# Hybrid decoder step with a product-key expert layer: expert weights through a table in device memory instead of one-hot matrix products

## The chip, the cores and the metric

One core of a Trainium2 chip. The time is device microseconds of one execution. The kernel before took 1174.33 us, the median of three runs (1173.85 to 1175.8).

## The reference

The reference is one layer of a decoder for 256 prompt tokens and 8 sample tokens: attention beside a state-space branch, an output projection, and an expert layer (PEER). All but the last part is the same in both kernels. The expert layer is this, for each token `xb` and each of 8 heads:

```python
qh = (xb @ wq).reshape(c, PEER_HEADS, 2, PEER_QDIM // 2)
s = einsum('chid,hikd->chik', qh, sub_keys)            # two lists of 128 scores
sv, si = top_k(s, 16)                                   # 16 best of each list
cand = sv[:, :, 0, :, None] + sv[:, :, 1, None, :]      # 256 sums
best, bi = top_k(cand, 16)                              # 16 best sums
e = i1 * 128 + i2                                       # their expert numbers
g = softmax(best)
act = gelu(einsum('cd,chkd->chk', xb, u_emb[e]))
out = einsum('chk,chkd->cd', g * act, v_emb[e])
```

There are 128 x 128 = 16384 experts, each with a row of 1024 numbers in U (`u_emb`) and in V (`v_emb`). A token takes 8 x 16 = 128 of them.

## The kernel before

The program runs in blocks: first the token mixing (input projection by a ring of weight tiles, attention, the state-space scan, output projection), then, from about 300 us, the block of the expert layer, which is all that the change touches apart from some transfers.

**Prompt tokens are computed densely.** For the 256 prompt tokens the kernel doesn't gather expert rows. It multiplies all tokens by all of U, applies gelu, multiplies each result by a weight that is zero for experts which the token didn't choose, and multiplies by all of V. Expert number c x 128 + p stands in row c and partition p of `acts`, a buffer of 128 partitions by 128 rows by 256 tokens.

- *U sweep* (`up`, L1689): 128 rows, each 24 matrix products of 128 x 256. U arrives on SP's queue in 256 pieces of 256 KB (two a row) in a ring of 8 places. Each piece is split into a rounded high half and the rest: ScalarE makes the high half (`high`, L1805), GpSimd the low one by a subtraction (`low`, L1567), in `hl`, which has four places. So ScalarE can be no more than four pieces ahead of TensorE. ScalarE then applies gelu to the row (L1872).
- *V sweep* (`down`, L1719): 32 groups of four rows, each 48 products of 128 x 512 which add up in four banks. V comes in 8 pieces a group. GpSimd makes six of the low halves and VectorE two (L2092). The weighted `acts` rows are split too, by ScalarE (L1901) and VectorE (`parts`, L2085).

**The search** is VectorE's. It takes the 16 best of 128 and then the 16 best of 256, head by head (`choose`, `top16`, L1978 to L1988), for both tiles of 128 tokens at once, then a ninth time for the sample tokens. A last stage (L2003 to L2031) turns the positions into expert numbers and the scores into softmax weights for all nine heads together; the exponential is ScalarE's, put behind row 44 of the sweep (L1891). From row 60 of the U sweep on (`R0`), TensorE turns these numbers so that a token is a column (L1774), and then works a group of four tokens (`TG`) after each row of U:

- VectorE (`one_hots`, L2047 and L2051) compares the numbers of each token with 0 to 127 and gets two 128 x 128 matrices, one for the low half of the expert number, one for the high half times the weight;
- TensorE (`route`, L1699) multiplies the two, which gives the dense 128 x 128 weights of the token, for four tokens in a bank;
- VectorE (`weigh`, L2060) multiplies the rows of `acts` that exist already, ScalarE keeps the rest for later rows (`keep`), and VectorE weighs each later row as it comes (`finish`, L2068).

The 64 groups go with rows 60 to 123. When all is weighted, TensorE adds the residual (L1739) and starts the V sweep. Sample tokens are done apart: their rows of U and V are fetched by 16 indirect gathers of 128 rows, issued by GpSimd in groups 12 to 15 and 21 to 24 of the V sweep (L1577).

## Time and profile before

| | |
|---|---|
| median of three runs | 1174.33 us (1173.85 to 1175.8) |
| the profiled execution, first to last instruction | 1177.8 us |
| TensorE busy | 1145.5 us |
| VectorE busy | 793.4 us |
| GpSimd busy | 758.9 us |
| ScalarE busy | 569.8 us |
| U sweep, first product to the last | 381.5 to 802.8 us |
| V sweep | 807.5 to 1171.3 us |

The profile is of one execution, and no time of it other than its span is given; the span is 3.5 us above the median. Engines in it: PE is TensorE, DVE VectorE, ACT ScalarE, POOL GpSimd, SP the engine that issues most transfers. "L1719" is line 1719 of the kernel. A timeline row gives start, duration, engine, line, operation, output and input, and in brackets how long the engine had been idle and what ended that.

### The profile page before, as it was taken

The numbers are of one execution on the slowest core, as the hardware profiler recorded it, in microseconds if no ns is written. First come the engines' busy times: TensorE is split into PE (matmuls) and PEld (weight loads), VectorE is DVE, ScalarE is ACT, GpSimd is POOL, SyncE is SP. The second block draws the span as 40 slices with busy tenths as digits, with TensorE's granted clock in tenths as the row PEclk, the third lists the DMA queues.
The fourth block names the chain that finished last, engine by engine and source line by source line (L and its number), as shares of the span: only waits on it lengthen the run. The fifth ranks groups of instructions, "written<-read, shape, count | busy, mean of one in ns | idle before, by whom it ended". The sixth has DMA issues, their size and how long they took to land.

```text
span 1177.8 us, 24286 instructions
## 1 busy us (share of the span) xinstructions
PE 1145.5 (97%) x7599; PEld 1012.2 (86%) x7599; DVE 793.4 (67%) x1718; ACT 569.8 (48%) x1289; POOL 758.9 (64%) x642
## 2 busy tenths in 40 slices
PE   8999999989999999999999999999999999999997
PEld 7887777758888999999999999998888887888876
DVE  6789788874299997002899999984454466665534
ACT  3323223544354555565555554445555555555545
POOL 0066443237355998988666666676677797789754
PEclk9999999999999999999999999999999999999999
DMA  7468667695443666656544455545666697788653
GB/s 249 143 231 280 195 194 221 207 344 175 152 155 109 199 186 185 187 172 189 143 144 139 141 143 144 144 143 153 187 188 189 189 325 252 224 281 291 191 153 108
DMA packets 108667, 225.13 MB, mean 191 GB/s; under 512 B 12754, under 2 KB 21570, under 8 KB 108074
## 3 DMA queue, kind: packets, MB, share of 16 engines
q1 hardware_dynamic: 104706, 210.50, 57.5%
q0 software_dynamic: 2944, 10.49, 2.6%
q10 hardware_dynamic: 936, 3.14, 0.7%
q8 instruction: 41, 0.67, 0.3%
q14 instruction: 40, 0.33, 0.1%
HBM read 215.80 MB, written 8.19 MB: 190 GB/s over the span
## 4 chain that ended last, share of the span: by engine, by line
PE 71%; issue 1%; DVE 1%; POOL 0%; ACT 0%; DVEq 0%; POOLq 0%; ACTq 0%
PE bank L1689 31%; PE bank L1719 30%; PE bank L1699 5%; PE bank L1642 2%; PE bank L1654 1%; PE bank L1666 1%; DVE hl L2092 0%; PE bank L1739 0%; PE bank L1756 0%; POOL hl L1582 0%; DVE acts L2115 0%; PE bank L1747 0%; ACT acts L1925 0%; POOL hl L1567 0%; PE bank L1774 0%
## 5 line engine op out<-in xcount | busy, mean ns | idle before, releaser
L1567 POOL TENSOR_TENSOR hl<-ring,hl 128x512 fp32r<-128x512 f32 x448 | 585.5, 1317 | 187.5 <-ACT hl L1805 180.5
L1805 ACT CAST hl<-ring 128x512 fp32r<-128x512 f32 x512 | 317.1, 620 | 292.1 <-PE bank L1719 161.7
L1689 PE MATMUL bank<-split,hl 128*128 128x256 f32 x3072 | 378.5, 282 | 0.4 <-ACT hl L1805 0.3
L1689 PEld LDWEIGHTS bank<-split,hl 128*128 128x128 f32 x3072 | 366.3, 189 | 0.8 <-issue 0.5
L1719 PE MATMUL bank<-hl,split 128*128 128x512 f32 x1524 | 353.9, 394 | 1.9 <-DVE hl L2092 1.9
L1719 PEld LDWEIGHTS bank<-hl,split 128*128 128x128 f32 x1524 | 286.2, 188 | 69.7 <-DVE hl L2092 2.4
L533 PE MATMUL pj<-xn,ring 128*128 128x264 f32 x672 | 158.5, 392 | 0.7 <-ACT proj L824 0.7
L2085 DVE TENSOR_TENSOR split<-acts,split 128x256 fp32r<-128x256 f32 x128 | 128.3, 1028 | 40.0 <-ACT split L1901 37.0
L533 PEld LDWEIGHTS pj<-xn,ring 128*128 128x128 f32 x672 | 126.4, 192 | 24.7 <-issue 4.6
L2092 DVE TENSOR_TENSOR hl<-ring,hl 128x512 fp32r<-128x512 f32 x64 | 49.9, 779 | 115.6 <-ACT hl L1805 115.6
L2051 DVE TENSOR_SCALAR bv<-bkey,ig 128x130 f32<-128x130 f32 x256 | 86.0, 394 | 0.0
L2060 DVE TENSOR_TENSOR acts<-acts,bank 128x244 f32<-128x244 f32 (+31 forms) x64 | 66.3, 1035 | 19.7 <-PE bank L1699 19.4
L471 POOL TENSOR_TENSOR hs<-hs,dds 128x256 f32<-128x256 f32 x32 | 21.1, 689 | 87.8 <-DVE xdt L1266 45.7
L1872 ACT ACTIVATE acts<-bank 128x256 f32<-128x256 f32 (+31 forms) x124 | 40.9, 330 | 67.5 <-PE bank L1689 67.5
L1699 PE MATMUL bank<-bv,av 128*128 128x128 f32 x512 | 67.4, 275 | 0.0
L515 POOL TENSOR_TENSOR wo<-ring,wo 128x512 fp32r<-128x512 f32 x32 | 42.9, 1358 | 31.1 <-ACT wo L973 31.0
L1699 PEld LDWEIGHTS bank<-bv,av 128*128 128x128 f32 x512 | 62.4, 191 | 0.0
L1582 POOL TENSOR_TENSOR hl<-ring,hl 128x512 fp32r<-128x512 f32 x24 | 31.0, 1301 | 35.9 <-ACT hl L1815 35.8
L1901 ACT CAST split<-acts 128x256 fp32r<-128x256 f32 x128 | 51.2, 402 | 0.2 <-DVE acts L2068 0.2
L2068 DVE TENSOR_TENSOR acts<-acts,gtmp 128x256 f32<-128x256 f32 (+32 forms) x67 | 41.8, 624 | 8.4 <-ACT gtmp L1874 8.4
L2047 DVE TENSOR_TENSOR av<-bank,ig 128x512 f32<-128x512 f32 x64 | 43.4, 678 | 0.0
L1642 PE MATMUL bank<-split,hl 128*128 128x264 f32 x288 | 37.3, 288 | 0.0
(369 smaller groups left out, 1107.1 us busy)
## 6 DMA issues: line engine op xcount, KB each, us to landing
ring<-in_uv SPq DMA_DIRECT2D x256, 256.0 KB, 2.7
ring<-in_v_rows SPq DMA_DIRECT2D x256, 256.0 KB, 3.1
ring<-in_w_ring SPq DMA_DIRECT2D x76, 512.0 KB, 4.2
room<-in_cache_k SPq DMA_DIRECT2D x64, 128.0 KB, 2.8
hs<-in_state_ssm SPq DMA_DIRECT2D x8, 512.0 KB, 4.7
out_ssm_s<-hs SPq DMA_DIRECT2D x8, 512.0 KB, 6.3
acts<-x_rows SPq DMA_DIRECT2D x8, 512.0 KB, 4.7
room<-in_cache_v SPq DMA_DIRECT2D x12, 256.0 KB, 5.7
```

The costliest lines, as they stand in the source:

```text
L533: mm = nc.tensor.matmul(pj[i % 2][:, 0:NT], ring[:, s, k], (xg if i < 2 else xn)[:, k], start=(k == 0), stop=(k == KD - 1))
L1567: nc.gpsimd.tensor_tensor(hl[:, r % HL, 1], raw[:, r], hl[:, r % HL, 0].bitcast(F32), ALU.subtract).then_inc(lo_done, 1)
L1642: mm = nc.tensor.matmul(qb[s][:, 0:NT], hl[:, n % HL, m, k * P:(k + 1) * P], split[:, x, 4 * a + k], start=(a + kind + k == 0), stop=(a + ...
L1689: mm = nc.tensor.matmul(out, hl[:, r % HL, m, k * P:(k + 1) * P], split[:, x, kk, 0:TP], start=(kk == 0 and n == 0), stop=(kk == KD - 1 an ...
L1699: mm = nc.tensor.matmul(rb[m % 2][:, j * P:(j + 1) * P], av[:, m % 2, j], bv[:, m % 2, j, 0:P], start=True, stop=True)
L1719: mm = nc.tensor.matmul(acc[2 * k + half][:], split[:, p, 2 * s + a, k * P:(k + 1) * P], hl[:, r % HL, m], start=False, stop=False)
L1805: nc.scalar.copy(hl[:, r % HL, 0], raw[:, r]).then_inc(hi_done, 1)
L1901: nc.scalar.copy(split[:, g % 2, 2 * n, 0:TP], acts[:, g * GRP + n, :]).then_inc(wg_hi, 1)
L2051: hot = nc.vector.tensor_scalar(bv[:, m % 2, j], bkey[:, :, 0:BW // BR], ig[:, 0, at:at + 1], ig[:, 2, at:at + 1], ALU.is_equal, ALU.mult)
L2060: nc.vector.tensor_tensor(a, a, rb[m % 2][:].rearrange("p (t c) -> p t c", t=TG)[:, :, 0:R0 + m + 1], ALU.mult).then_inc(g_out, 1)
L2085: nc.vector.tensor_tensor(split[:, p, 2 * s + 1, 0:TP], acts[:, g * GRP + s, :], split[:, p, 2 * s, 0:TP].bitcast(F32), ALU.subtract).then ...
L2092: nc.vector.tensor_tensor(hl[:, r % HL, 1], raw[:, r], hl[:, r % HL, 0].bitcast(F32), ALU.subtract).then_inc(lo_dve, 1)
```

## The change

The dense weights are no longer computed by products. They are added up in a table `gates` in device memory: 16384 experts by 256 tokens of 4 bytes, 16.8 MB.

- *Clearing.* Behind the last 32 of the 52 tiles of the input projection ScalarE's queue issues a transfer of zeros, 512 KB each, in runs of 1 KB (`clear_gates`).
- *Search in two parts.* After head 4 VectorE makes expert numbers and weights of heads 0 to 4 (`gate_weights`), then goes on with heads 5 to 7, the sample tokens and their numbers and weights. The exponentials stand behind rows 13 and 60 (`EA`, `EB`). A token's place in the table is (number x 256 + token), in `slot`.
- *Scattering.* For each head, tile and one of its 16 choices GpSimd issues an indirect transfer which adds 128 numbers of 4 bytes (one a token) to the table: 8 x 2 x 16 = 256 transfers. The 16 of a head and tile wait until those of the head before have landed for this tile.
- *Low halves.* GpSimd makes only the first 32 of U's low halves (`PA`); the other 224 are VectorE's, two behind each step of the search from head 5 on, one at places, and from piece 152 on in a loop (`up_lows`). GpSimd scatters meanwhile.
- *Weighing.* Before each group of four rows in the V sweep, SP's queue reads the group's 512 KB of the table into `gt` (two places, runs of 1 KB), and VectorE multiplies the four rows at once. The first such read waits for all the scatters.
- Gone are `one_hots`, `route`, `keep`, `finish` and the turning of the prompt tokens' numbers; only the sample tokens' are still turned, after row 75 (`RT`).

```diff
-TG = 4
-NTG = TP // TG
+RZ = 4
...
-R0 = 60
-BR, BW = 5, 130
-C_ID, C_ONE, C_IOTA, C_LAST, C_ROPS, C_AM, C_CM = np.cumsum([0, P, P, P, NT, NT, 3 * P]).tolist()
+R0 = 64
+RT = 76
+HA = 5
+PA = 32
+EA, EB = 13, 60
...
+                def clear_gates(n):
+                    act.wait_ge(zeros_set, 1)
+                    rows = t["gates"].rearrange("(c p t) o -> p c (t o)", p=P, t=TP)[:, n * RZ:(n + 1) * RZ]
+                    act.dma_start(rows, zeros[:].unsqueeze(1).broadcast_to([P, RZ, TP])).then_inc(gates_zero, 16)
...
+                    if i >= N_IN - NKEY // RZ:
+                        clear_gates(i - N_IN + NKEY // RZ)
...
+                    stream(1, PA // RAW + 1)
+                    stream(PA // RAW + 1, RT // 4 - 1)
+                    sp.wait_ge(g_done, 2 * TT)
+                    sp.wait_ge(found_done, 4 * TT)
...
+                    def gate_tile(g):
+                        if g >= 2:
+                            sp.wait_ge(weighed, g - 1)
+                        rows = t["gates"].rearrange("(c p t) o -> p c (t o)", p=P, t=TP)[:, g * GRP:(g + 1) * GRP]
+                        sp.dma_start(gt[:, g % 2], rows).then_inc(gt_in[g % 2], 16)
...
+                    for k in range(TT):
+                        sp.wait_ge(scattered[k], 16 * TOPK * PH)
+                    gate_tile(0)
+                    gate_tile(1)
...
+                    def scatter(h, k):
+                        if h:
+                            pool.wait_ge(scattered[k], 16 * TOPK * h)
+                        for s in range(TOPK):
+                            nc.gpsimd.indirect_dma_start(t["gates"], bass.IndirectOffsetOnAxis(ap=slot[:, k, h, s:s + 1], axis=0),
+                                                         found[:, 2, k, h, s:s + 1], None, compute_op=ALU.add).then_inc(scattered[k], 16)
...
-                    with pool.Fori(0, N_U // RAW) as i:
+                    with pool.Fori(0, PA // RAW) as i:
                         for r in range(RAW):
                             low(i * RAW + r, r)
+                    pool.wait_ge(gates_zero, 16 * NKEY // RZ)
+                    for h in range(PH):
+                        if h in (0, HA):
+                            n = 1 if h == 0 else 2
+                            pool.wait_ge(g_done, TT * n)
+                            pool.wait_ge(slot_done, TT * n)
+                        for k in range(TT):
+                            scatter(h, k)
...
-                    def route(m):
-                        if m >= 2:
-                            pe.wait_ge(g_kept, m - 1)
-                        pe.wait_ge(g_b, m + 1)
-                        for j in range(TG):
-                            mm = nc.tensor.matmul(rb[m % 2][:, j * P:(j + 1) * P], av[:, m % 2, j], bv[:, m % 2, j, 0:P],
-                                                  start=True, stop=True)
-                        mm.then_inc(g_mm, 1)
...
+                    with pe.Fori(1, PA // RAW) as i:
                         for j in range(4):
-                            up(i, j)
-                    pe.wait_ge(found_done, 4)
-                    pe.wait_ge(g_done, 2)
+                            up(i, j, lo_done, 0)
+                    with pe.Fori(PA // RAW, RT // 4) as i:
+                        for j in range(4):
+                            up(i, j, lo_dve, PA)
...
+                    with pe.Fori(RT // 4, NKEY // 4) as i:
+                        for j in range(4):
+                            up(i, j, lo_dve, PA)
+                    pe.wait_ge(ig_done, 1)
...
+                        if row == EA:
+                            exps(1, slice(0, HA))
+                        if row == EB:
+                            exps(2, slice(HA, PH + 1))
...
+                        act.wait_ge(weighed, g + 1)
...
+                    def up_lows(n):
+                        for m in range(spare_low[0], spare_low[0] + n):
+                            dve.wait_ge(hi_done, m + 1)
+                            nc.vector.tensor_tensor(hl[:, m % HL, 1], raw[:, m % RAW], hl[:, m % HL, 0].bitcast(F32), ALU.subtract
+                                                    ).then_inc(lo_dve, 1)
+                        spare_low[0] += n
...
+                        choose(P, h, range(TT), lambda k, side: scp[:, 2 * h + side, k], 0 if h < HA else 2)
+                        if h == HA - 1:
+                            gate_weights(slice(0, HA), True, 0)
...
+                    choose(hb, PH, range(1), lambda k, side: scs2[0:hb, side], 1)
+                    gate_weights(slice(HA, PH + 1), False, 2)
+                    up_lows(2 * RT - spare_low[0])
...
-                    def one_hots(m):
-                        if m >= 2:
-                            dve.wait_ge(g_mm, m - 1)
-                        ts = slice(m * TG, (m + 1) * TG)
-                        nc.vector.tensor_tensor(av[:, m % 2], akey.unsqueeze(1).broadcast_to([P, TG, P]),
-                                                ig[:, 1, ts].unsqueeze(2).broadcast_to([P, TG, P]), ALU.is_equal)
-                        for j in range(TG):
-                            at = m * TG + j
-                            hot = nc.vector.tensor_scalar(bv[:, m % 2, j], bkey[:, :, 0:BW // BR], ig[:, 0, at:at + 1],
-                                                          ig[:, 2, at:at + 1], ALU.is_equal, ALU.mult)
-                        hot.then_inc(g_b, 1)
...
+                    def weigh(g, p):
+                        dve.wait_ge(gelu_done, g * GRP + GRP)
+                        dve.wait_ge(gt_in[p], 16 * (g // 2) + 16)
+                        rows = acts[:, g * GRP:(g + 1) * GRP, :]
+                        nc.vector.tensor_tensor(rows, rows, gt[:, p], ALU.mult).then_inc(weighed, 1)
...
+                        if g < NG - 1:
+                            weigh(g + 1, 1 - g % 2)```

How the order of instructions moves, at three places. TensorE, end of the U sweep; before, `bv` and `av` are the two one-hot matrices of four tokens:

```order
L1699 MATMUL bank<-bv,av 128x128 x4
L1689 MATMUL bank<-split,hl 128x256 x24
L1699 MATMUL bank<-bv,av 128x128 x4
L1689 MATMUL bank<-split,hl 128x256 x96
L1739 MATMUL bank<-cst,res 128x128 x16
L1787 UNCONDITIONAL_BRANCH
```

and with the change (L1739 is now the product of `up`, L1779 the residual):

```order
L1739 MATMUL bank<-split,hl 128x256 x8
L1736 REGISTER_ALU
L1739 MATMUL bank<-split,hl 128x256 x4
L1814 REGISTER_ALU
L1814 COMPARE_AND_BRANCH
L1779 MATMUL bank<-cst,res 128x128 x16
```

The four products of a token group are gone from behind each of 64 rows, and the sweep is a loop to its end.

GpSimd between the low halves of U and those of V, with the change:

```order
L1601 TENSOR_TENSOR hl<-ring,hl 128x512
L1626 REGISTER_ALU
L1626 COMPARE_AND_BRANCH
L1609 DMA gates<-found,slot 4194304x1 x256
L1613 UNCONDITIONAL_BRANCH
L1613 ISA
L1601 TENSOR_TENSOR hl<-ring,hl 128x512
```

Before, the loop of V's low halves (L1571) follows directly on that of U's (L1584). Now the 256 scatters stand between them, and U's loop ends after 32 pieces.

VectorE between the first part's weights and head 5, with the change:

```order
L2073 TENSOR_REDUCE acts<-found 128x2x5
L2074 RECIPROCAL acts<-acts 128x2x5
L2076 TENSOR_TENSOR found<-found,acts 128x80 x2
L2008 MAX acts<-acts 128x8 x4
L2002 TENSOR_TENSOR hl<-ring,hl 128x512 x2
L2010 MAX_INDEX acts<-acts 128x8 x4
L2002 TENSOR_TENSOR hl<-ring,hl 128x512 x2
L2012 MATCH_REPLACE acts<-acts 128x128 x4
L2002 TENSOR_TENSOR hl<-ring,hl 128x512 x2
```

Two low halves (L2002) now stand behind each step of heads 5 to 7, 24 a head; before, head 5 followed on head 4 and the low halves were on GpSimd.

## Rows read from the trace of the kernel before

**Rows 1.** The page: span, and busy time of each engine

```profile
span 1177.8 us, 24286 instructions
...
PE 1145.5 (97%) x7599; PEld 1012.2 (86%) x7599; DVE 793.4 (67%) x1718; ACT 569.8 (48%) x1289; POOL 758.9 (64%) x642
```

**Rows 2.** Windows: length, busy us (PE, PEld, DVE, ACT, POOL), PEclk, DMA share, GB/s

```profile
100.00:226.00 126.00, 120.18 (x759) 95.20 (x757) 104.47 (x287) 40.87 (x142) 48.53 (x71) 1.00 0.69 221
450.00:500.00 50.00, 50.00 (x428) 50.00 (x427) 13.57 (x6) 27.11 (x54) 45.09 (x36) 1.00 0.65 185
600.00:650.00 50.00, 50.00 (x432) 50.00 (x432) 45.26 (x96) 27.18 (x69) 34.76 (x27) 1.00 0.47 143
...
940.00:985.00 45.00, 43.08 (x186) 34.62 (x186) 27.82 (x24) 24.02 (x47) 39.14 (x32) 1.00 0.87 295
```

**Rows 3.** Timeline (start us, us, line, shapes) of TensorE: first row, first routed rows

```profile
381.46 2.74 PE L1689 MATMUL bank<-split,hl 128*128 128x256 f32 x18 [0.26 <-ACT hl L1805]
...
551.16 0.38 PE L1774 MATMUL bank<-cst,acts 128*128 128x128 f32 x2
...
552.74 3.12 PE L1689 MATMUL bank<-split,hl 128*128 128x256 f32 x24
...
556.51 3.08 PE L1689 MATMUL bank<-split,hl 128*128 128x256 f32 x24
...
563.96 3.08 PE L1689 MATMUL bank<-split,hl 128*128 128x256 f32 x24
```

**Rows 4.** Timeline of VectorE: first maxima of heads 0 and 5; the weights' stage

```profile
330.18 0.86 DVE L1978 MAX8 acts<-acts 128x8 f32<-128x128 f32 x4
...
384.08 0.87 DVE L1978 MAX8 acts<-acts 128x8 f32<-128x128 f32 x4
...
425.11 0.46 DVE L2003 TENSOR_TENSOR acts<-acts 128x288 f32<-128x288 f32 x1
...
461.19 2.55 DVE L2024 TENSOR_REDUCE acts<-acts 128x144 f32<-128x2304 f32 x1
```

**Rows 5.** Timeline of ScalarE: a table load ahead of the exponential

```profile
509.97 1.28 ACT L1891 ACT_TABLE_LOAD   x1
```

**Rows 6.** Groups of the V sweep: busy us, mean ns, idle before

```profile
L1567 POOL TENSOR_TENSOR hl<-ring,hl 128x512 fp32r<-128x512 f32 x189 | 252.8, 1346 | 89.8 <-ACT hl L1805 83.0
...
L2085 DVE TENSOR_TENSOR split<-acts,split 128x256 fp32r<-128x256 f32 x124 | 126.9, 1048 | 39.4 <-ACT split L1901 36.4
L1901 ACT CAST split<-acts 128x256 fp32r<-128x256 f32 x124 | 49.8, 402 | 0.0
L2092 DVE TENSOR_TENSOR hl<-ring,hl 128x512 fp32r<-128x512 f32 x63 | 49.2, 780 | 115.6 <-ACT hl L1805 115.6
...
L2098 DVE TENSOR_TENSOR acts<-acts 128x1024 f32<-128x1024 f32 x8 | 9.7, 1217 | 0.0
L1577 POOL DMA_INDIRECT acts<-in_v_rows,eidx x8 | 9.5, 1187 | 1.2 <-issue 0.3
L1577 POOL DMA_INDIRECT acts<-in_u_rows,eidx x8 | 9.2, 1147 | 1.2 <-issue 0.6
```

**Rows 7.** The indirect gathers: ns min/median/max, time to landing

```profile
L1577 POOL DMA_INDIRECT acts<-in_u_rows,eidx x8: 957/1096/1463, 942.0 to 983.2; - x8
...
DMA to landing us min/median/max: 4.9/6.3/8.1
```

**Rows 8.** Timeline of TensorE: end of the U sweep, start of the V sweep

```profile
794.79 8.04 PE L1689 MATMUL bank<-split,hl 128*128 128x256 f32 x67
803.87 3.84 PE L1739 MATMUL bank<-cst,res 128*128 128x128 f32 x32 [1.05 <-DVE acts L2068]
807.47 22.72 PE L1719 MATMUL bank<-hl,split 128*128 128x512 f32 x97
```

**Rows 9.** DMA issues: KB each, median us from issue to landing

```profile
acts<-x_rows SPq DMA_DIRECT2D x8, 512.0 KB, 4.7
...
acts<-in_g_fin SPq DMA_DIRECT2D x1, 512.0 KB, 6.4
```

267 lines of the change are left out of this document (125 added, 142 removed).

## The prediction, made before the changed kernel ran

> **What bounds the kernel now.** I read the page first: TensorE is busy for 1145.5 of 1177.8 us, the others for two thirds or less [rows 1]. An average can hide stages, so the windows come next. Between 450 and 500 us, in the plain part of the U sweep, TensorE is busy for 50.00 of 50 us at full clock, and between 600 and 650, in the part with the one-hot products, again for 50.00, while VectorE has 45.26 [rows 2]. So every product taken out of the U sweep shortens it, as long as nothing else becomes the last to finish. The span is 3.5 us above the median of 1174.33; all terms below are differences within this execution, and I apply their sum to the median.
>
> **What is removed.** Plain rows: 60 of them lie between 381.46 and 551.16 [rows 3], 2.83 us each. Routed rows: three lie between 552.74 and 563.96, 3.74 each. The four products of a token group thus cost 0.91 us, and 64 groups 58 us. The turning of numbers takes 1.58 us (551.16 to 552.74); its three small products that stay are some 0.5, which saves 1. Together -59. VectorE's comparisons and weighings in this stage go too, but are worth nothing by themselves: TensorE never waited there.
>
> **The first deadline: VectorE's search.** Head 0 starts at 330.18, head 5 at 384.08 [rows 4], 10.8 us a head. The last stage for nine heads runs from 425.11 to 461.19 + 2.55, 38.6 us; five heads of nine take less than 25, mostly by size, so VectorE is through at about 408. It then waits for the exponential behind row 13: 381.46 + 14 x 2.83 = 421.1, then a table load of 1.28 [rows 5] and the function. Weights are ready at about 424.5. TensorE wants low half 32, VectorE's first, with row 16, at 381.46 + 16 x 2.83 = 426.7. One step of the search (0.9) and one subtraction stand before it, which just does. From there a head is 10.8 us of search and 24 low halves of 0.78 [rows 6], 29.5 us, for which TensorE takes 12 x 2.83 = 34: enough. The second weights' stage is tighter. Four ninths of 38.6 is 17, with chains and waits 18, and its 16 low halves 12.5; together 30 where TensorE needs 22.6, and only three pieces (4 us) can lie ready. I put +3 for it; 0 and +7 are the ends. What waits behind VectorE there is TensorE, through the low halves. The exponential is split in two, a second pair of table loads; ScalarE is busy for 27 of 50 us [rows 2], and they hide.
>
> **The second deadline: the scatters.** With 128 x 2.83 = 362, 0.6 for turning and the 3 above, the U sweep ends at 747. VectorE's last low half is done some 3 us before (the high half can be three pieces, 4.2 us, ahead, less the making of both), and then SP would read the first tile of the table: at 744.6. GpSimd starts at 424.5, and a landing takes 6.3 us [rows 7], so a scatter may cost (744.6 - 6.3 - 424.5) / 256 = 1.23 us of GpSimd. Nothing in the trace scatters or adds. The nearest rows are the gathers, which also make 128 transfers from a list in SBUF: 0.96 us at least and 1.46 at most [rows 7], with means of 1.15 and 1.19 [rows 6]. I take 1.17, since the work of the instruction is a list of the same length. That is 300 us: done at 724, landed at 730, 14 us to spare. So I cost the scatters at nothing; the cover is the U sweep, and each 0.1 us above 1.23 costs 26 us, since GpSimd, VectorE, ScalarE and TensorE all stand behind the first tile. The second part's 96 scatters find their weights ready: those come at about row 64, 563 us, and the first 160 scatters end at 424.5 + 187 = 612.
>
> The Trainium skill, SBUF — State Buffer, section Who interferes with whom, says that a VectorE instruction with two SBUF inputs and a GpSimd instruction that reads SBUF shut each other out for their whole length. The trace agrees as far as it goes: half as large as the low half's, `parts`' subtraction takes longer, 1.048 against 0.780 us, beside a GpSimd that is busy for most of the sweep [rows 6]. The scatters read their list from SBUF beside VectorE's low halves, so this rule speaks against the change; what it does here is the second rival below, worked out from gather rows.
>
> **Between the sweeps.** Before, 4.64 us pass from the last product of U (794.79 + 8.04 = 802.83) to the first of V at 807.47 [rows 8], of which the residual hides 3.84. Now a chain: tile of 512 KB read at 2.4 us before the end of U, landing after 4.7 to 6.4 [rows 9], multiplication of 1024 columns 1.22, cast 0.40, subtraction 1.05 [rows 6]. First product of V 5.0 to 6.7 us after the last of U: 0 to +2, I take +1.
>
> **The clearing.** 32 x 512 KB are written between about 100 and 226 us, 133 GB/s beside 221 GB/s at a share of 0.69 [rows 2]. At full share that rate would be 320, and the sum asked for is 354, 11% more: 13 us if all of it were on the path. But TensorE is busy for 120.18 of 126 us there and the weight ring is four tiles deep, so most of the delay should be absorbed. Ends 0 and +16, I take +5.
>
> **The V sweep.** It gains a multiplication of 1.22 us per group on VectorE and 512 KB of reads. VectorE: 1.22 + 2 x 0.78 + 4 x 1.05 = 7.0 of 11.3 us a group, fine. GpSimd: 6 x 1.35 = 8.1, and 1.22 if it is held off; fine too, except in the eight groups with two gathers each, where 8.1 + 2.4 + 1.2 = 11.7 is 0.4 too long. In the first four of these the DMA share is 0.87 at 295 GB/s and TensorE idles for 2 of 45 us already [rows 2]; the tile adds 46 GB/s, to about 1.0. Ends 0 and +12, I take +4.
>
> **Sum.** -59 + 3 + 1 + 5 + 4 = -46, so 1174.3 - 46 = 1128. With all ends low it is 1115, with all high 1152.
>
> **Rivals.**
>
> *The scatters come a little late* (chance 0.12). The gathers also have idle time ahead of them, 1.2 us for each eight [rows 6], 0.15 each, which may stay in a row of scatters. At 1.17 + 0.15 = 1.32 us a scatter they end at 762, 768 landed, 24 us late: 1152. For it speaks that a scatter may need the same preparation as a gather; against it that this may be done while the one before runs.
>
> *GpSimd needs far more per scatter, and the kernel gets slower* (0.15). Place: the wait of SP for `scattered`. If each scatter takes as long as the longest gather, 1.46, and the 0.15 in between, 1.61 x 256 = 412, landed at 843: 98 us late, 1226. It decides from 1.23 + 46 / 256 = 1.41 us. For it: the longest gathers are those next to a VectorE subtraction, and here VectorE makes one low half each 1.4 us; an added number also needs its old value read, perhaps more list to write. Against: the mean of 16 gathers under the same conditions is 1.17.
>
> *The DMA engines need too long for 32768 numbers of 4 bytes* (0.10). The U stream has a share of 0.65 [rows 2] at 185 GB/s, in runs of 2 KB: 115 ns of one engine each. If a small addition costs as much, 32768 x 115 ns / 16 = 235 us of all engines, on top of 0.65 x 300 = 195: 430 us of work in 300. 130 late less the 14 spare: 1128 + 116 = 1244. The point from which it decides is 0.35 x 300 + 14 + 46 = 165 us, 80 ns each. Against: a run 500 times shorter should not take as long.
>
> *The small terms all come high* (0.08): 1152, as above, from contention in the first stage and in the gather groups.
>
> *The change doesn't do what it says*, in that the products were hidden: excluded, TensorE was full in these rows.
>
> **Chances and range.** The forecast has 0.55, for 1115 to 1145; the two smaller gains 0.20; the two slower cases 0.25, of which a part lies near their points of decision. About 0.2%, 2.3 us, is what a measurement of this kernel can tell from no change. Faster 0.72: the forecast and nearly all of the smaller gains; same 0.03; slower 0.25. The range holds the forecast from a little below its low end, the smaller gains, and slower cases up to 1205, where a scatter costs 1.53 us: 1112 to 1205.
>
> **What would show it right or wrong.** In the profile after: the U sweep's products from 381 + some 5 to 750 at 2.83 us a row; scatters of about 1.17 us in two runs from 425, the last before 740; SP's wait for the first tile short; at most 7 us from the last product of U to the first of V; no TensorE waits for VectorE's low halves but some at rows 57 to 66. It is wrong if the last scatter stands behind the end of the U sweep, if the rows of U become longer than 2.83 (DMA or VectorE), or if the block of the token mixing grows by more than 16 us.

## The result, and the profile after

The change makes the kernel slower: 1309.99 us, the median of four runs (1308.65 to 1310.06), against 1174.97 (1173.85 to 1175.8) beside them; a ratio of 1.114, 95% interval 1.1125 to 1.1157. The forecast was 1128, its range 1112 to 1205. The profiled execution took 1310.05 us; the time from its first to its last instruction, its span, is 1308.4.

The page of the kernel after (span, busy time of each engine, TensorE's busy tenths and granted clock in 40 slices, the chain that ended last, costly groups):

```profile
span 1308.4 us, 22444 instructions
...
PE 1098.5 (84%) x7081; PEld 959.5 (73%) x7081; DVE 794.9 (61%) x1550; ACT 547.8 (42%) x1165; POOL 900.2 (69%) x674
...
PE   9999999899999999999999800000999998999997
...
PEclk9999999989999999999999955555999999999999
...
POOL 33%; PE 29%; issue 8%; DVE 5%; DMA 1%; ACT 1%; DVEq 0%; POOLq 0%; ACTq 0%; SPq 0%
POOL gates L1609 31%; PE bank L1759 21%; PE bank L1739 3%; DVE split L2115 2%; PE bank L1692 2%; PE bank L1704 1%; POOL hl L1601 1%; DVE hl L2122 1%; DMA ring<-in_v_rows 1%; PE bank L1716 1%; DVE acts L2128 0%; ACT hl L1838 0%; DVE acts L2109 0%; DMA gt<-gates 0%; DVE hdot L2129 0%
...
L1609 POOL DMA_INDIRECT gates<-found,slot x256 | 409.4, 1599 | 80.6 <-issue 78.4
...
L1739 PE MATMUL bank<-split,hl 128*128 128x256 f32 x3072 | 364.2, 280 | 1.9 <-DVE hl L2002 1.4
...
L2115 DVE TENSOR_TENSOR split<-acts,split 128x256 fp32r<-128x256 f32 x128 | 145.6, 1161 | 27.7 <-ACT split L1924 25.0
...
L2109 DVE TENSOR_TENSOR acts<-acts,gt 128x1024 f32<-128x1024 f32 x32 | 44.4, 1388 | 177.0 <-DMA gt<-gates 177.0
```

In [rows 1] TensorE was busy for 97%; now for 84%, with a hole of five slices (a slice is 32.7 us) in which only GpSimd works, and the chain goes through the scatters (L1609) for 31% of the span. A scatter takes 1.599 us on average, and GpSimd idles for another 80.6 us ahead of them, 0.31 each.

The timeline of GpSimd in the hole, when nothing else runs (shown: two of them); a start each 1.855 us:

```profile
800.14 1.55 POOL L1609 DMA_INDIRECT gates<-found,slot  x1 [0.30 <-issue]
802.00 1.55 POOL L1609 DMA_INDIRECT gates<-found,slot  x1 [0.30 <-issue]
```

The view of the tile `gates`, all transfers on it (ns min/median/max, first and last start):

```profile
L1609 POOL DMA_INDIRECT gates<-found,slot x256: 1545/1550/2066, 423.2 to 909.5; - x128
L831 ACTq DMA_DIRECT2D gates<-zeros x32: 366/394/760, 65.4 to 221.8; - x32
L1546 SPq DMA_DIRECT2D gt<-gates x32: 375/434/919, 912.5 to 1264.1; - x32
...
  issue: 78.4, 255
```

From 423.2 to 909.5 there are 255 steps of 1.907 us. The timeline around both sweeps, TensorE first (start of U, end of U, residual, start and end of V), then what stands between the last scatter and V:

```profile
378.62 2.61 PE L1739 MATMUL bank<-split,hl 128*128 128x256 f32 x17 [0.26 <-ACT hl L1838]
...
739.74 4.98 PE L1739 MATMUL bank<-split,hl 128*128 128x256 f32 x41
744.55 3.74 PE L1779 MATMUL bank<-cst,res 128*128 128x128 f32 x32
918.76 6.45 PE L1759 MATMUL bank<-hl,split 128*128 128x512 f32 x21 [170.47 <-DVE split L2115]
...
1298.88 2.96 PE L1772 MATMUL bank<-hl,split 128*128 128x512 f32 x12
```

```profile
909.49 1.55 POOL L1609 DMA_INDIRECT gates<-found,slot  x1 [0.30 <-issue]
...
912.54 0.94 SPq L1546 DMA_DIRECT2D gt<-gates  x2
...
916.45 1.23 DVE L2109 TENSOR_TENSOR acts<-acts,gt 128x1024 f32<-128x1024 f32 x1 [175.73 <-DMA gt<-gates]
...
917.77 1.32 ACT L1924 CAST split<-acts 128x256 fp32r<-128x256 f32 x4 [172.12 <-DVE acts L2109]
...
918.21 1.43 DVE L2115 TENSOR_TENSOR split<-acts,split 128x256 fp32r<-128x256 f32 x4 [0.53 <-ACT split L1924]
```

These answer to [rows 3, 8]. From them the difference of the two spans, 1308.4 - 1177.8 = 130.6 us, is accounted for:

| stretch | before | after | difference |
|---|---|---|---|
| up to the first product of U | 381.5 | 378.6 | -2.8 |
| U sweep, first product to the last | 421.4 | 366.1 | -55.3 |
| last of U to first of V | 4.6 | 174.0 | +169.4 |
| V sweep, to its last product | 363.8 | 383.1 | +19.3 |

The gain came as expected; the wait for the scatters takes three times as much, and V loses 19 us. The medians differ by 135.0 us, 4 more than the spans. Where time and span of an execution are both given, the span is about 1.7 us shorter, so the profiled execution of the kernel before was some 5 us above its median (an estimate); the differences taken from its trace carry that with them. The experiments ask what a scatter pays for, and what V pays for.

### The profile page after: what moved, and what is told of

It is laid out like the page before. It is cut to its first block, busy times and chain, and to the rows that moved or that the text cites. A ratio compares the mean times of both kernels' runs of the same rounds, so it can differ in the third digit from the quotient of the medians.

```text
span 1308.4 us, 22444 instructions
## 1 busy us (share of the span) xinstructions
PE 1098.5 (84%) x7081; PEld 959.5 (73%) x7081; DVE 794.9 (61%) x1550; ACT 547.8 (42%) x1165; POOL 900.2 (69%) x674
## 2 busy tenths in 40 slices
PE   9999999899999999999999800000999998999997
## 4 chain that ended last, share of the span: by engine, by line
POOL 33%; PE 29%; issue 8%; DVE 5%; DMA 1%; ACT 1%; DVEq 0%; POOLq 0%; ACTq 0%; SPq 0%
POOL gates L1609 31%; PE bank L1759 21%; PE bank L1739 3%; DVE split L2115 2%; PE bank L1692 2%; PE bank L1704 1%; POOL hl L1601 1%; DVE hl L2122 1%; DMA ring<-in_v_rows 1%; PE bank L1716 1%; DVE acts L2128 0%; ACT hl L1838 0%; DVE acts L2109 0%; DMA gt<-gates 0%; DVE hdot L2129 0%
## 5 line engine op out<-in xcount | busy, mean ns | idle before, releaser
L1759 PE MATMUL bank<-hl,split 128*128 128x512 f32 x1524 | 363.6, 401 | 181.9 <-DVE split L2115 170.5
L1759 PEld LDWEIGHTS bank<-hl,split 128*128 128x128 f32 x1524 | 290.9, 192 | 254.8 <-issue 171.5
L1609 POOL DMA_INDIRECT gates<-found,slot x256 | 409.4, 1599 | 80.6 <-issue 78.4
L1838 ACT CAST hl<-ring 128x512 fp32r<-128x512 f32 x512 | 316.1, 618 | 253.7 <-PE bank L1759 171.5
L1601 POOL TENSOR_TENSOR hl<-ring,hl 128x512 fp32r<-128x512 f32 x224 | 320.7, 1457 | 97.9 <-ACT hl L1838 93.8
L1739 PE MATMUL bank<-split,hl 128*128 128x256 f32 x3072 | 364.2, 280 | 1.9 <-DVE hl L2002 1.4
L1739 PEld LDWEIGHTS bank<-split,hl 128*128 128x128 f32 x3072 | 361.9, 188 | 4.1 <-DVE hl L2002 2.9
L2115 DVE TENSOR_TENSOR split<-acts,split 128x256 fp32r<-128x256 f32 x128 | 145.6, 1161 | 27.7 <-ACT split L1924 25.0
L2109 DVE TENSOR_TENSOR acts<-acts,gt 128x1024 f32<-128x1024 f32 x32 | 44.4, 1388 | 177.0 <-DMA gt<-gates 177.0
L1924 ACT CAST split<-acts 128x256 fp32r<-128x256 f32 x128 | 51.1, 402 | 173.4 <-DVE acts L2109 173.4
L2101 DVE TENSOR_TENSOR hl<-ring,hl 128x512 fp32r<-128x512 f32 x104 | 71.6, 692 | 71.1 <-ACT hl L1838 44.3
L2122 DVE TENSOR_TENSOR hl<-ring,hl 128x512 fp32r<-128x512 f32 x64 | 66.0, 1032 | 69.2 <-ACT hl L1838 69.2
L2002 DVE TENSOR_TENSOR hl<-ring,hl 128x512 fp32r<-128x512 f32 x120 | 82.8, 695 | 39.0 <-ACT hl L1838 23.6
L1904 ACT ACTIVATE acts<-bank 128x256 f32<-128x256 f32 x128 | 49.2, 384 | 90.9 <-PE bank L1739 60.3
L1624 POOL TENSOR_TENSOR hl<-ring,hl 128x512 fp32r<-128x512 f32 x24 | 30.9, 1297 | 36.0 <-ACT hl L1848 35.8
L1692 PE MATMUL bank<-split,hl 128*128 128x264 f32 x288 | 37.3, 287 | 0.0
L1692 PEld LDWEIGHTS bank<-split,hl 128*128 128x128 f32 x288 | 35.3, 188 | 2.0 <-issue 2.0
L837 ACT COPY proj<-pj 128x264 f32<-128x264 f32 x42 | 15.5, 370 | 42.0 <-PE pj L540 41.3
## 6 DMA issues: line engine op xcount, KB each, us to landing
ring<-in_w_ring SPq DMA_DIRECT2D x76, 512.0 KB, 5.2
gates<-zeros ACTq DMA_DIRECT2D x32, 512.0 KB, 5.8
gt<-gates SPq DMA_DIRECT2D x32, 512.0 KB, 5.0
hs<-in_state_ssm SPq DMA_DIRECT2D x8, 512.0 KB, 6.1
out_ssm_s<-hs SPq DMA_DIRECT2D x8, 512.0 KB, 7.6
```

The costliest lines, as they stand in the source:

```text
L1601: nc.gpsimd.tensor_tensor(hl[:, r % HL, 1], raw[:, r], hl[:, r % HL, 0].bitcast(F32), ALU.subtract).then_inc(lo_done, 1)
L1609: nc.gpsimd.indirect_dma_start(t["gates"], bass.IndirectOffsetOnAxis(ap=slot[:, k, h, s:s + 1], axis=0), found[:, 2, k, h, s:s + 1], None, ...
L1692: mm = nc.tensor.matmul(qb[s][:, 0:NT], hl[:, n % HL, m, k * P:(k + 1) * P], split[:, x, 4 * a + k], start=(a + kind + k == 0), stop=(a + ...
L1739: mm = nc.tensor.matmul(out, hl[:, r % HL, m, k * P:(k + 1) * P], split[:, x, kk, 0:TP], start=(kk == 0 and n == 0), stop=(kk == KD - 1 an ...
L1759: mm = nc.tensor.matmul(acc[2 * k + half][:], split[:, p, 2 * s + a, k * P:(k + 1) * P], hl[:, r % HL, m], start=False, stop=False)
L1838: nc.scalar.copy(hl[:, r % HL, 0], raw[:, r]).then_inc(hi_done, 1)
```

## The experiments

**What a scatter pays for.** My first theory was that the accumulation costs GpSimd time; its rivals were the length of the list, the short pieces in device memory, and the DMA engines. Four runs ask for them. A run that is given with one time was executed once.

*b_half*: half of the scatters. It leaves out the last 8 of the 16 choices of each head, that is half of the weights.

```diff
-                        for s in range(TOPK):
+                        for s in range(TOPK // 2):
```

> Edit: only 8 of the 16 choices of each head and tile are scattered, 128 transfers instead of 256; the other half of the expert weights is left out of the table. Theory A (GpSimd's making of each transfer, 1.55 us and a gap of 0.30, is the bound, and everything behind the U sweep waits for the last one): the scatters end at 423 + 128 x 1.9 = 666 us, before the end of the U sweep at 745, so the gap between the sweeps falls from 174 us to about 6 and the time from 1310 to 1310 - 168 = 1142, faster than before the change; each transfer still takes 1.55 + 0.30 us. Rival B (the DMA engines, not GpSimd, set the pace): each transfer of half as many would be shorter, well under 1.5 us. Rival C (something else than the scatters holds the first tile of the table): the gap stays well above 6 us. The V sweep stays at about 383 us by every theory, as it does not depend on the scatters.

1137.43 us (1136.93 to 1140.37) against 1173.59: ratio 0.970, 95% interval 0.968 to 0.972. The last scatter starts at 673.4, V's first product at 751.11, right behind the residual at 747.62. So the hole is the scatters' alone. It also shows what the rest of the change is worth, with the scatters free: -36 us, not the -46 of my sum. (The spans of the two traces differ by 42.5, for the reason given above.)

*c_plain*: the transfers write instead of adding, so an expert which two heads of a token chose keeps one weight of the two.

```diff
-    found[:, 2, k, h, s:s + 1], None, compute_op=ALU.add)
+    found[:, 2, k, h, s:s + 1], None)
```

> Edit: the 256 transfers write instead of adding; an expert chosen by two heads keeps only one weight. If the adding is what makes a scatter dearer than a gather (1.85 us from one to the next, against 0.96 + 0.16 for the gathers of the same run), it falls to about 1.15 us, the last stands at 423 + 256 x 1.15 = 717 us and the time is about 1142. If writing to device memory by a list costs that much in itself, it stays at 1.85 us and the time at 1310.

*d_part64*: lists of 64 numbers instead of 128; the weights of every second 64 tokens are left out.

```diff
-nc.gpsimd.indirect_dma_start(t["gates"], bass.IndirectOffsetOnAxis(ap=slot[:, k, h, s:s + 1], axis=0),
-    found[:, 2, k, h, s:s + 1], None, compute_op=ALU.add)
+nc.gpsimd.indirect_dma_start(t["gates"], bass.IndirectOffsetOnAxis(ap=slot[0:P // 2, k, h, s:s + 1], axis=0),
+    found[0:P // 2, 2, k, h, s:s + 1], None, compute_op=ALU.add)
```

> Edit: the transfers add only the numbers of partitions 0 to 63, 256 transfers of 64 numbers; the weights of the other tokens of each tile are left out. If a transfer's price is by the length of its list, it falls from 1.55 to about 0.8 us and the distance to about 1.1 (705 us for the last, time about 1142). If it is a fixed price of the instruction, it stays at 1.55 + 0.30 and the time at 1310. Between the two, the difference gives both parts.

*e_gather*: 4-byte fetches from the same places of the table, in place of the scatters; all weights are left out.

```diff
-nc.gpsimd.indirect_dma_start(t["gates"], bass.IndirectOffsetOnAxis(ap=slot[:, k, h, s:s + 1], axis=0),
-    found[:, 2, k, h, s:s + 1], None, compute_op=ALU.add)
+nc.gpsimd.indirect_dma_start(gt[:, k, 0, s:s + 1], None, t["gates"],
+    bass.IndirectOffsetOnAxis(ap=slot[:, k, h, s:s + 1], axis=0))
```

> Edit: the 256 transfers go the other way, each fetches 128 numbers of 4 bytes from the table into a buffer that is overwritten later; nothing is added to the table, so the expert weights are all zero. If the direction is what costs, a transfer takes 0.96 us and stands 1.12 from the next, as the gathers of 4 KB rows do, and the time is about 1142. If such short pieces cost GpSimd more than rows of 4 KB, or a row of indirect transfers can't follow each other faster, it is 1.85 and 1310.

The three took 1182.07, 1286.03 and 1178.49 us. The view of the tile `gates` of each, c_plain first, then d_part64, then e_gather:

```profile
L1609 POOL DMA_INDIRECT gates<-found,slot x256: 952/962/1477, 425.8 to 781.4; - x128
```

```profile
L1609 POOL DMA_INDIRECT gates<-found,slot x256: 1412/1416/1912, 424.7 to 888.1; - x128
```

```profile
L1609 POOL DMA_INDIRECT gt<-gates,slot x256: 938/947/1459, 424.1 to 778.2; - x128
```

A write takes 0.962 us of GpSimd, a fetch 0.947, an addition 1.550, in the median: **adding costs 0.59 us**. In the row as it stands, beside VectorE for most of it, the distance from one start to the next is 1.907 us with additions and 1.394 with writes, 0.51 more. A list half as long saves 0.13 of 1.55, so the length, which I had priced by, hardly counts: some 2 ns an entry. Direction counts for nothing, and neither does the shortness of the pieces: the shortest gather of whole rows took 0.957 [rows 7]. In all four an idle 0.30 us stands between one transfer and the next. So even 0.96 + 0.30 = 1.26 is above my threshold of 1.23, and c_plain's average is 1.394: its last transfer starts at 781.4, and V waits 39 us.

The pages also count packets on the queue of GpSimd's transfers. Taken by the transfer, an adding one is 144 packets of 4 bytes (80 with the list of 64), a writing or fetching one 32, of 32 and of 4 bytes. So an addition is also a longer piece of work for whoever writes these packets. By d_part64, 64 packets fewer are worth 0.13 us; at that price the 112 between adding and writing would be 0.24 of the 0.59 (an estimate). What the rest pays for stays open.

The DMA engines were not the limit. In windows of the hole (us, then busy time of PE, PEld, DVE, ACT, POOL, then granted clock, DMA share, GB/s), of after and then of c_plain:

```profile
800.00:850.00 50.00, 0.00 (x0) 0.00 (x0) 0.00 (x0) 0.00 (x0) 41.80 (x27) 0.50 0.22 0
```

```profile
755.00:780.00 25.00, 0.00 (x0) 0.00 (x0) 0.00 (x0) 0.00 (x0) 19.01 (x20) 0.50 0.02 0
```

27 scatters of 128 additions, 0.22 of 16 engines' 50 us: 176 / 3456 = 51 ns an addition, where 80 ns was the point from which my rival of the DMA engines decided. For a write the same sum gives some 3 ns (0.02 x 16 x 25 / 2560), where eight numbers share a packet. So an addition is dear there too, but U's stream had room: its rows stayed at full speed.

**What V pays for.** V lost 13.8 us in b_half too (377.6 from first to last product, against 363.8), so most of it isn't the late start. Theory L is VectorE's multiplication with GpSimd's interference, the rival the reads of the table. Both with half of the scatters, as b_half. The length of V differs between executions: the one kernel of m_all_half, q_half_again and r_half_many, below, has 377.9, 379.5 and 383.2 us.

*f_nomul*: the multiplication is cut to one number per partition; the weights are left out.

```diff
-    nc.vector.tensor_tensor(rows, rows, gt[:, p], ALU.mult).then_inc(weighed, 1)
+    nc.vector.tensor_tensor(rows[:, 0, 0:1], rows[:, 0, 0:1], gt[:, p, 0, 0:1], ALU.mult).then_inc(weighed, 1)
```

> Edit, on the kernel with 128 scatters: the multiplication of four rows is cut to one number, the reads of the table stay; the expert weights are left out. It asks why the V sweep lasts 377.6 us there against 363.8 before. Theory L (VectorE's extra 1.2 us a group pushes its subtractions beside GpSimd's, where they wait, so its last low half of a group comes late): the V sweep falls to about 365 us and the time to about 1125. Rival D (the table's 512 KB a group on the DMA engines): it stays at 377.

*g_noread*: only the first two tiles of the table are read; all groups are multiplied by these.

```diff
-                            if i + 1 < NG:
-                                gate_tile(i + 1)
...
-                        dve.wait_ge(gt_in[p], 16 * (g // 2) + 16)
+                        dve.wait_ge(gt_in[p], 16)
```

> Edit, on the kernel with 128 scatters: only the first two tiles of the table are read and used for all groups, the multiplications stay; the expert weights are wrong from the third group on. Theory L: the V sweep stays at about 377 us. Rival D: it falls to about 365 us. If each has a share, both this and the run without the multiplication lie between.

1127.15 and 1136.14 us. V takes 366.5 us without the multiplication and 379.6 without the reads, against 377.6 in b_half. So the multiplication is worth 11 us, and no cost of the reads shows: 2 us the other way is within what executions of one kernel differ by. What TensorE waited for in V (us in total, times, longest), in b_half, f_nomul and g_noread, where L2120 is L2122:

```profile
PE bank L1759 <- DVE hl L2122: 9.9, 6, 3.8
```

```profile
PE bank L1759 <- DVE hl L2122: 3.1, 1, 3.1
```

```profile
PE bank L1757 <- DVE hl L2120: 10.2, 6, 2.7
```

It waits for VectorE's low half. The two longest waits of b_half, 3.8 and 3.6 us, and the one of f_nomul lie in groups with gathers. The timeline of such a place in the kernel after, ScalarE (ACT), VectorE (DVE) and GpSimd (POOL):

```profile
1079.46 0.62 ACT L1838 CAST hl<-ring 128x512 fp32r<-128x512 f32 x1 [1.41 <-DMA ring<-in_v_rows]
...
1080.43 0.43 DVE L2115 TENSOR_TENSOR split<-acts,split 128x256 fp32r<-128x256 f32 x1 [1.23 <-ACT split L1924]
1080.50 1.18 POOL L1619 DMA_INDIRECT acts<-in_u_rows,eidx  x1 [0.16 <-issue]
...
1081.25 9.39 DVE L2115 TENSOR_TENSOR split<-acts,split 128x256 fp32r<-128x256 f32 x3 [0.40 <-ACT split L1924]
1081.70 3.79 POOL L1601 TENSOR_TENSOR hl<-ring,hl 128x512 fp32r<-128x512 f32 x3
...
1085.65 0.96 POOL L1619 DMA_INDIRECT acts<-in_u_rows,eidx  x1 [0.16 <-issue]
1086.63 3.72 POOL L1601 TENSOR_TENSOR hl<-ring,hl 128x512 fp32r<-128x512 f32 x3
...
1090.51 0.95 POOL L1619 DMA_INDIRECT acts<-in_u_rows,eidx  x1 [0.16 <-issue]
1090.57 0.68 DVE L2122 TENSOR_TENSOR hl<-ring,hl 128x512 fp32r<-128x512 f32 x1
...
1091.30 4.87 PE L1759 MATMUL bank<-hl,split 128*128 128x512 f32 x13 [3.67 <-DVE hl L2122]
```

Three of VectorE's subtractions (L2115), 1.161 us each on average, take 9.39 us: one by one 4.53, 0.41 and 4.60. GpSimd goes from three subtractions to a gather to three subtractions with hardly a gap. The first and the third of VectorE's start beside a gather and are held until GpSimd's run of three behind it ends; the low half that stands behind them comes at 1090.57, and TensorE, which had waited 3.67 us for it, goes on at 1091.30. By the Trainium skill, SBUF — State Buffer, section Who interferes with whom, a VectorE instruction with two inputs in SBUF and a GpSimd instruction that reads SBUF exclude each other for their whole length; the trace agrees with it, at 9.39 us for three. In the kernel before, at the same place, the two engines took turns:

```profile
943.49 4.20 POOL L1567 TENSOR_TENSOR hl<-ring,hl 128x512 fp32r<-128x512 f32 x3
943.70 4.61 DVE L2085 TENSOR_TENSOR split<-acts,split 128x256 fp32r<-128x256 f32 x4 [1.11 <-ACT split L1901]
...
948.23 0.68 DVE L2092 TENSOR_TENSOR hl<-ring,hl 128x512 fp32r<-128x512 f32 x1
```

Four in 4.61 us, 1.40, 1.44, 1.38 and 0.41 one by one, beside GpSimd's of 1.31, 1.50 and 1.48. So VectorE can get in behind each of GpSimd's subtractions, or only behind three. Subtractions of over 2.5 us: 1 of 128 before, 6 after, 7 in b_half, 6 in g_noread, 2 in f_nomul; most start beside a gather. Why it is now the one and now the other isn't shown, nor how the multiplication brings about more of the long ones. VectorE did not come late to the place above from work of its own: it waited 1.23 us for ScalarE's cast, and ScalarE 1.41 for a piece of V.

Another wait, of 2.16 us, lies in a group without gathers. There VectorE's own queue is too full. It has not only the multiplication in it but also the dot product of a sample token (`dot`, L2128 and L2129), which eight groups have. With the low halves (L2122) these are 2.31, 1.78, 2.31 and 1.22 us from 1125.93 on, and then:

```profile
1133.46 5.72 DVE L2115 TENSOR_TENSOR split<-acts,split 128x256 fp32r<-128x256 f32 x4
...
1134.77 4.13 POOL L1601 TENSOR_TENSOR hl<-ring,hl 128x512 fp32r<-128x512 f32 x3 [0.17 <-ACT hl L1838]
...
1139.11 0.68 DVE L2122 TENSOR_TENSOR hl<-ring,hl 128x512 fp32r<-128x512 f32 x1
...
1139.84 2.71 PE L1759 MATMUL bank<-hl,split 128*128 128x512 f32 x6 [2.16 <-DVE hl L2122]
```

That is 13.9 us of VectorE without a pause, for a group that TensorE works off in 11.1.

*h_order*: on b_half, the second low half of a group stands between the second and third subtraction instead of behind the fourth.

```diff
-                            parts(g + 1, 1 - g % 2)
+                            parts(g + 1, 1 - g % 2, 0, 2)
                         low(g, 1)
+                        if g < NG - 1:
+                            parts(g + 1, 1 - g % 2, 2, GRP)
```

> Edit, on the kernel with 128 scatters: VectorE makes the second low half of a group between its second and third subtraction of the next group's rows instead of behind the fourth. Theory L: the stalls of up to 3.8 us, each ended by that low half, go, the V sweep falls to about 366 us and the time from 1137.4 to about 1127. Rival D, or if GpSimd itself is late: no change, 377 us.

1132.92 us (1132.41 to 1134.43) against 1175.96: ratio 0.963, interval 0.9605 to 0.966. The median is 4.5 us below b_half's, and the two intervals of the ratio don't touch; I expected 10. V takes 374.6 us in this trace, 3 less, and TensorE still waits 8.5 us for L2122, with as many long subtractions (7) as in b_half. The order helps a little; most of what the multiplication costs remains.

**The two together, with all weights.** *i_first*: head 0's 32 transfers write and the others add. The table is zero there, so nothing is left out.

```diff
-    found[:, 2, k, h, s:s + 1], None, compute_op=ALU.add)
+    found[:, 2, k, h, s:s + 1], None, **({"compute_op": ALU.add} if h else {}))
```

> All 256 transfers, but those of head 0 (32 of them) write instead of adding: the table is zero there and a token's 16 choices in one head are 16 different places, so the sum is the same. Theory A (adding costs 0.59 us of GpSimd in each transfer, 1.55 against 0.96): the first 32 take 0.96 + 0.30 each, the last lands 32 x 0.59 = 19 us earlier, 1310 - 19 = 1291 us. Rival: the cost belongs to the stretch of transfers and not to the single one (adds of another head still under way slow the writes, or the reverse): the row of 32 is no shorter than 1.8 us each, 1310 us. In neither is it faster than the kernel before.

*j_both*: i_first with the order of h_order.

> i_first and in the V sweep the order of h_order (second low half between the second and third subtraction). Theory A with Theory L: 1291 less the 3 to 5 us which that order gave with half the transfers: 1286 to 1288, a ratio of 1.095. Rival: the V sweep's stalls behind a late start have another cause (the clock after 170 us of idling): the order gives nothing, 1291.

1289.49 us, and 1285.75 (1282.57 to 1288.19) against 1174.88, a ratio of 1.093, interval 1.090 to 1.0965. Both as Theory A said: the row of transfers is 21 us shorter, and the order gives 3.7, though that is within the 5.6 us by which j_both's own four times differ. Neither beats the kernel before.

**Something unforeseen, and four more kernels for it.** In i_first the U sweep took 412.8 us instead of 366.1 and ended 52 us later than in the kernel after, hidden behind the wait for the scatters (in j_both, 413.2). TensorE's timeline beside the writes; "issue" is idle time in which it waited for nothing that the profile shows:

```profile
461.87 0.37 PE L1739 MATMUL bank<-split,hl 128*128 128x256 f32 x1 [1.73 <-issue]
464.67 0.37 PE L1739 MATMUL bank<-split,hl 128*128 128x256 f32 x1 [2.42 <-issue]
466.77 0.37 PE L1739 MATMUL bank<-split,hl 128*128 128x256 f32 x1 [1.73 <-issue]
```

Single products, 2 to 3 us apart, where they had followed each other without a gap. VectorE, ScalarE and SP crawled too; only GpSimd kept its pace. In c_plain, with eight times as many writes, nothing of that is seen. So I varied which transfers write, on b_half's half of them.

*k_first_half* (head 0 writes), *l_last_half* (head 7 writes), *m_all_half* (all write); where a write meets a number of another head it replaces it. Their edits are on b_half, in this order:

```diff
-    found[:, 2, k, h, s:s + 1], None, compute_op=ALU.add)
+    found[:, 2, k, h, s:s + 1], None, **({"compute_op": ALU.add} if h else {}))
...
+    found[:, 2, k, h, s:s + 1], None, **({"compute_op": ALU.add} if h < PH - 1 else {}))
...
+    found[:, 2, k, h, s:s + 1], None)
```

> b_half (half of the transfers, the other half of the weights left out), with head 0's 16 transfers writing instead of adding. With the full number, the run with head 0 written showed something unforeseen: between 430 and 485 us TensorE, ScalarE and SP issued one instruction each 1 to 2 us, and the U sweep ended 52 us later, hidden there by the wait for the transfers. Theory M (the change from writing to adding within the kernel causes it): it returns here and is now on the path, up to 1137 + 50 = 1187 us. Rival N (it was an accident of those two runs, or needs the full number): 1137 less nothing, 1137 us, since the transfers are hidden anyway.

> b_half, with the last head's 16 transfers writing and the others adding (a weight of an expert which another head chose too is overwritten). Theory M: TensorE, ScalarE and SP slow down near the last head's transfers, about 640 to 680 us, by some tens of us: 1150 to 1187. Rival O (what matters is that the first transfers are writes, which come faster than adds): no slow stretch, 1137.

> b_half with all 128 transfers writing (an expert chosen twice keeps one weight). Theory M: no change of kind, no slow stretch, 1137, as with all 256 written the U sweep ended in time. Rival O: a slow stretch at the first transfers, as in the run with head 0 written, 1150 to 1187.

1152.27, 1149.10 and 1290.68 us, where b_half has 1137: each is slower, the more writes the more, and the crawl lies where the writes are (425 to 450 us in the first, with TensorE busy for 12.58 of 25; 650 to 700 in the second, 40.85 of 50). In the last TensorE waited 133.3 us for issue. The U sweep is longer than 366 us by 20, 13 and 156, for 16, 16 and 128 writes: some 0.8 to 1.3 us for each write, and in i_first 47 for 32, 1.5 each. Then on a second occasion, beside each other, *n_plain* (c_plain's kernel), *o_spaced* (m_all_half with a clearing of 128 numbers a partition behind each transfer) and *q_half_again* (m_all_half's kernel); the edit of o_spaced is

```diff
+                            nc.gpsimd.memset(fill[:], 0.0).then_inc(filled, 1)
+                            fills[0] += 1
+                            pool.wait_ge(filled, fills[0])
```

> The kernel of c_plain once more (all 256 transfers write; an expert chosen twice keeps one weight), beside m_all_half on the same chip: c_plain took 1182 us and its other engines ran undisturbed beside the writes; with 128 writes (m_all_half) they issued one instruction each 1 to 2.5 us and the kernel took 1291. Theory S (whether writes choke the other engines' issue differs from one placement of the program or chip to another, not with the number): here it is choked too, far above 1182, 1250 to 1500. Rival C (the code of c_plain differs in some way that protects it): 1182 again, with V's first product at 790.

> m_all_half with a small clearing of a buffer by GpSimd behind each written transfer, so that they stand further apart, about 1.6 to 1.9 us as adding ones do, where no choking was ever seen. Theory R (the rate of the transfers does it): little or no choking, 1137 to 1160 us. Rival K (the kind does it: writes, at any rate): choked as before, 1250 or more.

> m_all_half unchanged, as the control on this chip for the two others. If its choking belongs to the kernel: 1291 us within some tens. If it is chance from run to run: anywhere between 1137 and 1300.

1181.56, 1141.57 and 1138.98 us. The control did not crawl, so o_spaced tells nothing of rate or kind, and the same kernel has taken 1291 and 1139. Last, *r_half_many*, the same kernel again in six executions on one chip:

> The same kernel as m_all_half and q_half_again (128 transfers, all writing), which took 1291 us once and 1139 once, in several executions. If the choking belongs to the single execution: values of both kinds within this run. If it belongs to the chip or to where the program was loaded: all executions alike, at 1139 or all far above.

All six between 1289.8 and 1298.1 us, median 1295.11, with the kernel before at 1176.12 beside it. The window of 425 to 500 us in q_half_again, then in m_all_half (columns as above):

```profile
425.00:500.00 75.00, 75.00 (x640) 75.00 (x640) 59.34 (x179) 41.74 (x83) 57.66 (x53) 1.00 0.67 187
```

```profile
425.00:500.00 75.00, 19.14 (x98) 16.61 (x97) 9.30 (x36) 4.83 (x10) 57.03 (x60) 0.58 0.14 32
```

So the crawl is not chance from execution to execution: it belongs to the chip or to where the program and its table were placed. The record has the chip of each run: c_plain (chip 0) and n_plain and q_half_again (1) did not crawl, i_first and j_both (7), k_first_half, l_last_half and m_all_half (8) and r_half_many (11) did. No chip had a kernel with writes on two occasions, so chip and placement can't be told apart. The crawl comes beside writes that follow each other each 1.27 us. Additions, each 1.86, did not bring it on the same occasions: in l_last_half TensorE works at full pace beside them (from 430 to 550 us, busy for 120.00 of 120) until the writes of the last head, and in i_first, where they begin at 469.6, the crawl dies away in 20 us and from 490 to 550 us TensorE is busy for all of the time. In m_all_half's window the DMA share is 0.14, so it is not the DMA engines' time that is short. What is contended for stays open.

## Why the prediction was wrong

The step that failed is the price of a scatter: "I take 1.17, since the work of the instruction is a list of the same length". Measured are 1.60 on average and 0.31 in between, 1.91 in all, 0.68 above the threshold of 1.23; 256 times that is 174 us, where V's first product waited 170.5. Three things were wrong in it. The accumulation has a price of its own, 0.59 us (c_plain). The list's length, on which the likeness rested, is worth 0.13 for a halving (d_part64). And back to back there is a gap of 0.30 us, which I put in a rival, at 0.15, from the gathers' eight gaps [rows 6]. The runs part the two costs: with the scatters hidden 1137 (b_half), with writes at 1.07 on average and the gap 1182 (c_plain), with additions 1310. So a row of plain writes with its gap already costs 45 us and leaves no gain, and adding costs 128 more.

- **The slower rival** had the place (SP's wait for `scattered`) and the mechanism ("an added number also needs its old value read, perhaps more list to write"; the list is longer, 144 packets for 32), with a size too small: 1.61 us for 1.91, 1226 for 1310, since its upper bound was the longest gather [rows 7]. A bound from the longest instance of another operation was no bound.
- **The late-scatter rival** (1.32 us) fits the writes of c_plain: 1.394 from start to start.
- **The DMA engines' rival** was wrong in size, 51 ns for 115.
- **The one-hot products**: -59 with the turning forecast; measured -57, that is 55.3 which the sweep lost in spite of the 1.4 of the next point. U's rows took 2.82 us, with 2.83 forecast.
- **VectorE's second weights' stage**: +3 forecast; TensorE waited 1.4 us, in six waits, between 555 and 567 us (rows 62 to 65).
- **The first deadline**: weights ready at 424.5 forecast, the first scatter starts at 423.18.
- **The clearing**: +5 forecast (0 to 16), nothing measured; U starts 2.8 us earlier here and 0.2 later in b_half, and over all runs between 377.7 and 383.7. In the window of 100 to 226 us, TensorE does not suffer and the DMA share of [rows 2], 0.69, is full:

```profile
100.00:226.00 126.00, 122.56 (x851) 96.50 (x849) 100.49 (x286) 44.40 (x146) 45.76 (x69) 1.00 0.98 328
```

- **Between the sweeps**: the chain from the last scatter is the one that I wrote, read of the tile 3.9 us, multiplication 1.23, cast, subtraction; but SP could issue that read 1.5 us behind the last scatter's end, where I had 6.3. In b_half, with the chain hidden, 3.3 us pass from U to V, 1.3 less than before, for the +1.
- **The V sweep**: +4 forecast (0 to 12), +13.8 in b_half, +19.3 in the kernel after, of which 9.3 are TensorE's waits (11.2 against 1.9) and 9.7 longer products (363.6 us busy with L1759, 353.9 before): the window of the first four gather groups has a granted clock of 0.96 (shown in the last section), where [rows 2] had 1.00 in these groups. It falls just where TensorE goes on after its four longest waits, of 3.67, 2.16, 2.63 and 1.99 us: windows of 4 us from 1092, 1140, 1178 and 1215 on have a granted clock of 0.57, 0.57, 0.62 and 0.57. What they lack to 1.00 is 6.7 us, and V's start at the low clock adds 1.5 (918 to 922, at 0.54, busy 3.24): some 8 of the 9.7, an estimate. So each us of waiting cost about another in slower products. I had added GpSimd's time in a gather group (11.7 of 11.3 us) and left VectorE out as "fine", at 7.0. The sum left out the dot product of the eight groups that have one, 2.4 us [rows 6 for its first half], and the time for which GpSimd holds VectorE off. The lock which I weighed against the scatters decided here instead.

What the change is worth with the scatters hidden is then, in b_half's trace, -55.3 for U, +13.8 for V, -1.3 between them and +0.2 in front: -42.5 us of span, and -36 by the medians. To hide them, GpSimd would have to be through in 314 us, 1.23 a scatter, and no form of the transfer that I measured is as short: the cheapest two, 0.96 and 0.95 with 0.30 in between, need 1.39 on average beside VectorE. A mixture, with scatters for one tile of tokens and one-hot products for the other, would by b_half give about 1137 + 29 = 1166 us (an estimate; VectorE would have both kinds of work in the same rows). It wasn't tried.

## What to carry to other kernels

When work moves to an engine with time to spare, price the new instruction by what it does (here: adding), not by its size, and give the row of them its gaps; where one number times 256 decides the sign, and nothing in the trace is of that kind, the honest range is wider than the nearest neighbour's spread. An indirect transfer of 128 numbers costs GpSimd 1.26 us from start to start and an adding one 1.86, with little difference between lists of 64 and of 128: make few of them. And an engine's sum of busy times says "fine" only while no other engine holds it off: look at what stands in its queue in front of the instruction that the critical engine waits for, in the groups that have extra work above all.

## What was unexpected in the hardware

- An adding transfer costs 0.59 us more of GpSimd than a writing one, is 144 packets instead of 32, and takes 51 ns of a DMA engine for each 4-byte number instead of 3.
- With TensorE idle since 748 us the granted clock fell to 0.50, that is 1.2 GHz, as the window of the hole shows; V's first products started each 0.43 us, against 0.23 later. In the window of 1057 to 1102, with the wait of 3.67 in it, it is 0.96 on average:

```profile
1057.00:1102.00 45.00, 41.11 (x168) 32.06 (x167) 34.47 (x27) 21.54 (x43) 35.88 (x29) 0.96 0.91 317
```

- 16.8 MB of zeros in runs of 1 KB, written beside the weight stream, brought the traffic to 328 GB/s at a share of 0.98 without delaying a product.
- Rows of short writes can slow the issue of all other engines to one instruction in 1 to 3 us, on some occasions and not on others, for all executions of an occasion. So a kernel with many small indirect writes should be timed on more than one occasion.
